# One inference step of a hybrid decoder layer: in each attention step the key transposes go ahead of the probability transposes

## The reference, cut to what matters

```python
DILATED_BRANCHES = ((128, 1), (512, 4), (2048, 16))
...
s = jnp.einsum('bthd,btjhd->bhtj', q, kg).astype(jnp.float32) * ATT_SCALE + bias[None, :, None, :]
p, lse = masked_softmax_stats(s, valid[None, None])
outs.append(jnp.einsum('bhtj,btjhd->bthd', p.astype(vc.dtype), vg))
```

## Time and profile before

| | |
|---|---|
| time, median of 3 runs | 2128.72 us (2128.16 to 2460.03) |
| the profiled execution | 2129.07 us, its span 2127.3 us |
| PE matmul busy | 1966.9 us, 92% of the span |
| DVE busy | 1087.4 us, 51% |
| ACT busy | 452.8 us, 21% |
| mean granted TensorE clock | 0.975 |

### The profile page before, as it was taken

One profiled execution on the slowest core, in us unless ns is written; L12 is line 12 of the kernel. 1 busy time (PEld: TensorE's weight loads), 2 busy tenths in 40 slices (PEclk: granted clock), 3 DMA queues, 4 the chain that ended last, 5 costly groups with the idle time before them and its releaser, 6 DMA issues.

```text
span 2127.3 us, 33466 instructions
## 1 busy us (share of the span) xinstructions
PE 1966.9 (92%) x13165; PEld 1789.0 (84%) x13165; DVE 1087.4 (51%) x2114; ACT 452.8 (21%) x880; POOL 460.9 (22%) x250
## 2 busy tenths in 40 slices
PE   7999996889999599889989999999999999999987
PEld 6999894666666499889644999999999999999987
DVE  6698445767676433621441344454444444544555
ACT  5100122445444401410331112000000000000004
POOL 2332220000000021633000222332232332332330
PEclk9999998999999899999999999999999999999998
DMA  4499957798888611421126113234324423411102
GB/s 143 163 329 309 327 151 168 181 203 200 199 184 184 182 31 30 142 77 59 40 83 214 30 49 128 101 118 167 118 79 166 157 80 127 157 44 45 39 30 84
DMA packets 275626, 282.83 MB, mean 133 GB/s; under 512 B 12017, under 2 KB 258169, under 8 KB 273593
## 3 DMA queue, kind: packets, MB, share of 16 engines
q1 hardware_dynamic: 273357, 280.49, 44.4%
q10 hardware_dynamic: 2176, 1.05, 0.2%
HBM read 268.05 MB, written 113.89 MB: 180 GB/s over the span
## 4 chain that ended last, share of the span: by engine, by line
PE 56%; issue 5%; DVE 3%; POOL 1%; DMA 1%; ACT 1%; SPq 0%; DVEq 0%; POOLq 0%; ACTq 0%
PE bank L1294 25%; PE bank L1102 12%; PE bank L1312 11%; PE bank L1232 1%; PE bank L1208 1%; POOL w_lo L809 1%; PE bank L1251 1%; PE bank L1223 1%; PE bank L1336 0%; DVE accf L2235 0%; PE bank L1187 0%; DVE xT L2253 0%; DVE xm L2111 0%; DVE g_lo L2129 0%; PE bank L1114 0%
## 5 line engine op out<-in xcount | busy, mean ns | idle before, releaser
L789 POOL CAST w_hi<-w_raw 128x1024 fp32r<-128x1024 f32 x112 | 119.5, 1067 | 1552.7 <-PE bank L1102 681.3
L1294 PE MATMUL bank<-g_lo,w_hi 128*128 128x362 f32 (+1 forms) x1056 | 350.5, 332 | 0.0
L1294 PE MATMUL bank<-g_hi,w_lo 128*128 128x362 f32 (+1 forms) x1056 | 350.4, 332 | 0.0
L1294 PE MATMUL bank<-g_hi,w_hi 128*128 128x362 f32 (+1 forms) x1056 | 347.9, 329 | 1.5 <-DVE tmp0f L2185 1.5
L791 POOL TENSOR_TENSOR w_lo<-w_raw,w_hi 128x1024 fp32r<-128x1024 f32 x112 | 301.1, 2688 | 9.0
L1102 PE MATMUL bank<-g_hi,w_hi 128*128 128x362 f32 (+1 forms) x576 | 190.9, 331 | 15.3 <-DVEq L2008 9.2
L1294 PEld LDWEIGHTS bank<-g_hi,w_hi 128*128 128x128 f32 x1056 | 200.0, 189 | 1.7 <-DVE tmp0f L2185 1.6
L1294 PEld LDWEIGHTS bank<-g_hi,w_lo 128*128 128x128 f32 x1056 | 201.4, 191 | 0.0
L1294 PEld LDWEIGHTS bank<-g_lo,w_hi 128*128 128x128 f32 x1056 | 199.8, 189 | 0.0
L2253 DVE TENSOR_TENSOR xT<-bank,xT 128x362 f32<-128x362 f32 (+1 forms) x264 | 139.7, 534 | 115.9 <-PE bank L1312 115.9
L1102 PE MATMUL bank<-g_lo,w_hi 128*128 128x362 f32 (+1 forms) x576 | 192.1, 333 | 0.0
(11 more groups left out here) (283 smaller groups left out, 3304.1 us busy)
## 6 DMA issues: line engine op xcount, KB each, us to landing
out_sk_dram<-in_cache_win_k_dram SPq DMA_DIRECT2D x24, 2040.0 KB
out_sv_dram<-in_cache_win_v_dram SPq DMA_DIRECT2D x24, 2040.0 KB
vn<-in_cache_win_v_dram SPq DMA_DIRECT2D x48, 288.0 KB, 5.6
kb<-in_cache_win_k_dram SPq DMA_DIRECT2D x96, 128.0 KB, 4.0
vn<-in_cache_win_v_dram SPq DMA_DIRECT2D x48, 256.0 KB, 5.3
w_raw<-in_w_in_dram SPq DMA_DIRECT2D x22, 512.0 KB, 11.0
w_raw<-in_w_ffn_gate_dram SPq DMA_DIRECT2D x22, 512.0 KB, 3.8
w_raw<-in_w_ffn_up_dram SPq DMA_DIRECT2D x22, 512.0 KB, 3.8
```

Source lines behind the costliest of these rows:

```text
L789: pool.tensor_copy(w_hi[slot][:, :], w_raw[slot][:, :]).then_inc(w_hi_done, 1)
L1294: last = pe.matmul(out, w, r, start=start, stop=stop)
```

## The change

In PE's loop `turn_keys(u, 2 if second else 0)` now stands ahead of `turn_p(d - 1)`. So that the bank rotation agrees, the numbering in `FILL` is moved in the same way: `K2` or `K0` before `P`. `K1` stays at the end of the even step. The programs of ACT, DVE and SP are the same text; only the bank and the semaphore counts that they take from `FILL` differ.

```diff
         for d in range(STEPS):
             u, second = divmod(d, 2)
-            if d:
-                number("P", d - 1, 5)
             if second:
                 number("K2", u, 2)
+                if d:
+                    number("P", d - 1, 5)
                 if u:
                     number("OS", u - 1, 1)
...
             else:
                 number("K0", u, 4)
+                if d:
+                    number("P", d - 1, 5)
                 if u:
                     number("PS", u - 1, 3)
                 number("K1", u, 4)
...
             for d in range(STEPS):
                 u, second = divmod(d, 2)
+                turn_keys(u, 2 if second else 0)
                 if d:
                     turn_p(d - 1)
-                turn_keys(u, 2 if second else 0)
                 if u and not second:
                     turn_sample_p(u - 1)
                 scores(d)
```

## The result

The changed kernel takes 2191.12 us (median of 4 runs, 2188.09 to 2192.90) against 2128.53 us (median of 4). It is slower by 62.6 us, with a ratio of 1.0296 and a 95% interval of 1.0277 to 1.0315. One of the runs of the kernel before, 2460.03 us, stands far off the others and takes no part in the ratio. The profiled execution has a span of 2191.1 us, 63.8 more than before.

A forecast was written before the change was run, and what follows sets the result against it. The prediction took PE, by its order and waits, to bound the kernel. Losses of 13.5 + 24.0 + 3.0 = 40.5 us, plus 9 for the clock, made 49.5 us, so 2178 us, range 2160 to 2200.

The forecast's parts named there:

- What bounds the kernel: PE leads the touched stage, 328 of 373 us; `turn_p`'s input is long ready, so turning keys first fills no gap.
- Even steps without `bias_rows`: Six steps: `K0` no longer covers ACT's sample exponential, so sample transposes come 2.25 us late; 13.5 us in all.
- Even steps with it: Five steps: keys hold the three banks while DVE is in `bias_rows`; sample transposes 4.8 us late, 24.0 us in all.
- The small waits of `turn_p` for DVE: Sign expected in the profile after: small waits of L996 for DVE `kt`; no size given.
- Odd steps: Eleven steps with `K2` ahead of `turn_p`: put at nothing, with ends of 0.8 loss and 0.3 gain a step.
- This stays hidden: Key loads, wanted 2.49 us sooner, cost nothing; if not hidden, they would cost the 2.5 us again.
- The step of the sum that named the margin: Loads: tightest is `K2` of unit 4, landing at 473.8, wanted at 474.4 plus the even step's 4.8 us lateness.
- the rival: A key load becomes late: each of eleven odd steps waits up to 2.5 us more; 2192 likelier, chance 0.05.
- Step d = 1: PE waits first for the late `K2` load and does `turn_p` behind it: a loss of 3.0 us.
- The clock: 16 new idle stretches in even steps, 6 of 11 lowering the clock at 1.0 us each: 9 us.
- the upper bound that the prediction gave: Clock term if all 16 new idle stretches lower the clock at 1.5 us each: 24 us.
- The upper end that it pointed to: Rival that every new wait lowers the clock: 40.5 + 24 = 64.5 us, so 2193; chance 0.12.

The follow-up runs named there:

- the two edits that undo the covers: Changed kernel with ACT making the sample exponential before its `turn_p` copies and DVE making the `K0` copies ahead of `bias_rows`; both together 2135.7 us.
- the odd half alone: Kernel before with only `K2` moved ahead of `turn_p`, in odd steps, and even steps as before; 2139.1 us, ratio 1.0037.
- short even steps: Changed kernel with early sample exponential, `K0` copies ahead of `bias_rows`, and DVE's `K1` copies right behind the prompt scores' biases; 2126.0 us.

## Why the prediction was right, and where its sizes were off

- **What bounds the kernel.** As read: PE, by its order and its waits. `turn_p` never waited for its input, so the new order filled nothing.
- **Even steps without `bias_rows`.** Predicted 2.25 us each, from hand-worked fills and copies; the sample transposes come 2.32 us later in their step. The predicted wait of about 2.2 us is 2.18.
- **Even steps with it.** Predicted 4.8 us; the trace has 4.85 in steps d = 8 and d = 4. Predicted wait at the fourth fill 2.76, measured 2.65. By the two edits that undo the covers, 55 us of the loss hang on these two steps of the sum, the clock's part included. The small waits of `turn_p` for DVE that were named as a sign do not show in the changed kernel.
- **Odd steps.** Predicted as nothing; 0.1 us in all. But the number was in part luck: six steps are 0.15 us longer, twice the 0.07 worked out, and a wait of `values` in d = 7 that no edit touches fell from 1.3 to 0.4 us. "This stays hidden" holds only as long as the even steps are late; in the odd half alone two loads are late, and with short even steps five are. The step of the sum that named the margin had the right mechanism; the rival deserved more than its 0.05.
- **Step d = 1.** Predicted 3.0, measured 3.8 for the first two steps together. `turn_p` ran wholly at the lower level (3.95 us), where I had let the clock come back on the way.
- **The clock.** This term was mis-sized, and it is the step of the prediction that failed. Predicted 9 us: 16 new idle stretches, of which the share of 6 in 11 costs 1.0 us each through the clock. The even steps grew by 54.2 us; 6 x 2.32 and 5 x 4.85 are 38.2 of these, which leaves 16 for the clock, and further 1 and 6 us came at the end of the stage and behind it. The kernels with filled idle time say the same in another way: 62.6 less 38.4 is 24 us, the upper bound that the prediction gave. Two readings failed. The share: the falls at new waits lie in the five steps with `bias_rows`, in each of them, and none lies at the new wait of the six steps without it; and more of the old waits have one. In the changed kernel all eleven even steps have a fall behind the `K1` wait, where 6 of 11 had before. Five of the six steps without `bias_rows` now have one and the same length, 20.55 or 20.56 us, with the fall at the same place; why the share rose stays open. And the price: a fall costs 1.0 to 1.7 us, as the 2.61 us for transposes that took 1.65 show, and the 3.85 us for `values` that took 2.19. A step without `bias_rows` takes 20.55 us with its fall and 18.9 with the idle time filled, so nothing of the 1.65 us is hidden under DVE's pace.
- **What I took from the Trainium skill's rule on PSUM-queue depth-cycling.** The upper end that it pointed to, 64.5 us, comes closer to the 62.6 measured than my choice. The trace does not bear it out in each place, as not every new wait is followed by a fall (the transposes after the exponential in d = 10 take 1.42 us, at full clock); the sum is met by fewer falls at new waits, of greater price, and by more of the old ones.
- **What counts as a change.** The prediction took 2%, 42.6 us, for about the least that can be told from nothing. The intervals here are some 0.2% to either side, and ratios of 1.0028 and 0.9969 are told from 1.

## What to carry to other kernels

Before moving work ahead of other work on the busiest engine, look at what the moved piece covered where it stood: here 2 us of transposes lay exactly over another engine's exponential, and the row that proved it was the one place in the kernel where the cover was missing. When two kinds of work share a few banks in turn, the order decides whose reader must be free first; put the kind first whose reader is not busy. If a wait can't be avoided, its cost has a second part, the clock. And look at the reader's order too: here four copies ahead of the inverse sums won 25 us, where the new order of the producer only lost.

## What the runs showed of the hardware

- Filling idle time with transposes that nobody reads made two kernels faster: 2191.1 to 2160.5 us, and 2129.9 to 2122.1. In the first the waits ended at the same time, and what rose was the granted clock of the stage, from 0.90 to 0.98.
- The idle time before the fourth `K1` fill, 2.28 to 2.46 us, was followed by a fall of the clock in 6 of 11 even steps of one kernel and in all 11 of another. In the latter, the 2.18 us of idle time before the sample transposes was followed by none in the six steps without `bias_rows`. The length of the idle time alone doesn't tell; what else decides it no run here isolates.
- The same code behind the stage took 1400.7 to 1407.3 us in thirteen traces, so a change of a few microseconds in one trace says nothing by itself.
